# An encoder with four attention mixers in fp32: B's two softmax maps are combined before the transposes, and the small TensorE instructions are issued one at a time between the dense matmuls

## The reference

```python
def block(args):
    qblk, pblk = args
    sc = jnp.einsum('bqmhd,bsmhd->bmhqs', qblk, k) * scale
    dist = jnp.abs(pblk[:, :, None] - posf[:, None, :])
    sc = sc - slopes[None, None, :, None, None] * dist[:, None, None]
    a = jax.nn.softmax(sc, axis=-1)
    a = a[:, 0] - lam[None, :, None, None] * a[:, 1]
    return jnp.einsum('bhqs,bshv->bqhv', a, v)
o = rms_norm(o, subln_g) * (1.0 - lam_init)
```

## Time and profile before

| | us |
|---|---|
| median of 3 runs | 3001.43 |
| lowest and highest | 2998.47, 3010.02 |
| profiled execution, device time | 3004.72 |
| its span | 3002.9 |
| PE busy in it | 2820.7 |
| DVE busy, ACT busy | 1566.0, 1179.0 |
| mean granted TensorE clock | 0.978 |

### The profile page before, as it was taken

One profiled execution on the slowest core, in us unless ns is written; L12 is line 12 of the kernel. 1 busy time (PEld: TensorE's weight loads), 2 busy tenths in 40 slices (PEclk: granted clock), 3 DMA queues, 4 the chain that ended last, 5 costly groups with the idle time before them and its releaser, 6 DMA issues.

```text
span 3002.9 us, 44753 instructions
## 1 busy us (share of the span) xinstructions
PE 2820.7 (94%) x13358; PEld 2267.0 (75%) x13358; DVE 1566.0 (52%) x3238; ACT 1179.0 (39%) x2387; POOL 0.6 (0%) x5
## 2 busy tenths in 40 slices
PE   5999989989989998999979999898899899999998
PEld 4889978666667887888868898776666678788887
DVE  5454476444445445555644544764354454465655
ACT  4444444434433234332434444534444332342432
POOL 0000000000000000000000000000000000000000
PEclk9999999889999999999989999999999999999999
DMA  4212222001112332333332122220111123223332
GB/s 152 72 48 72 78 63 85 12 29 41 45 37 78 94 96 78 99 98 99 99 100 64 44 78 79 67 85 1 36 43 50 31 91 98 92 85 98 95 96 91
DMA packets 141819, 217.62 MB, mean 72 GB/s; under 512 B 14777, under 2 KB 69387, under 8 KB 141195
## 3 DMA queue, kind: packets, MB, share of 16 engines
q1 hardware_dynamic: 132521, 200.62, 21.4%
q10 hardware_dynamic: 9058, 14.06, 1.4%
HBM read 206.20 MB, written 8.45 MB: 71 GB/s over the span
## 4 chain that ended last, share of the span: by engine, by line
PE 81%; DVE 9%; ACT 4%; issue 4%; ACTq 1%; DMA 1%; DVEq 0%; SPq 0%
PE bank L452 21%; PE bank L454 20%; PE bank L453 20%; PE bank L665 7%; PE bank L655 6%; PE bank L503 5%; DVE s_work L1563 1%; DVE s_wl L1139 1%; ACT s_wh L776 1%; ACT s_work L1027 1%; DVE s_work L1294 1%; PE bank L539 1%; ACTq L874 1%; DMA s_raw<-in_w_in 0%; ACT s_work L1019 0%
## 5 line engine op out<-in xcount | busy, mean ns | idle before, releaser
L1139 DVE TENSOR_TENSOR s_wl<-s_raw,s_wh 128x1024 fp32r<-128x1024 f32 (+2 forms) x372 | 453.6, 1220 | 526.5 <-ACT s_wh L776 525.9
L776 ACT ACTIVATE s_wh<-s_raw 128x1024 fp32r<-128x1024 f32 (+2 forms) x372 | 392.2, 1055 | 625.1 <-PE bank L454 591.9
L452 PE MATMUL bank<-s_hTh,s_wh 128*128 128x512 f32 x1216 | 486.2, 400 | 4.5 <-DVE s_work L1231 4.5
L454 PE MATMUL bank<-s_hTh,s_wl 128*128 128x512 f32 x1216 | 476.9, 392 | 0.0
L453 PE MATMUL bank<-s_hTl,s_wh 128*128 128x512 f32 x1216 | 476.7, 392 | 0.0
L452 PE MATMUL bank<-s_wh,s_hTh 128*128 128x512 f32 (+1 forms) x1088 | 475.8, 437 | 0.0
L454 PE MATMUL bank<-s_wh,s_hTl 128*128 128x512 f32 (+1 forms) x1088 | 427.0, 392 | 0.0
L453 PE MATMUL bank<-s_wl,s_hTh 128*128 128x512 f32 (+1 forms) x1088 | 426.7, 392 | 0.0
L1019 ACT ACTIVATE s_work<-s_work,s_stat 128x128 f32<-128x128 f32 (+3 forms) x384 | 214.1, 558 | 369.5 <-DVE s_stat L1588 123.0
L1563 DVE COPY s_work<-bank 128x256 f32<-128x256 f32 (+1 forms) x288 | 105.2, 365 | 394.5 <-ACT s_work L1027 391.9
L503 PE MATMUL bank<-s_consts,s_work 128*128 128x128 f32 (+1 forms) x1560 | 250.0, 281 | 47.3 <-DVE s_gTl L1495 14.3
(11 more groups left out here) (166 smaller groups left out, 3199.6 us busy)
## 6 DMA issues: line engine op xcount, KB each, us to landing
s_raw<-in_w_in SPq DMA_DIRECT2D x168, 512.0 KB, 3.4
s_raw<-in_ffn_w_up SPq DMA_DIRECT2D x176, 256.0 KB, 2.9
s_raw<-in_ffn_w_down SPq DMA_DIRECT2D x44, 512.0 KB, 3.7
s_raw<-in_w_branch SPq DMA_DIRECT2D x32, 512.0 KB, 3.6
s_raw<-in_w_o SPq DMA_DIRECT2D x16, 512.0 KB, 3.6
x_keep<-s_work ACTq DMA_DIRECT2D x2, 2048.0 KB, 7.5
s_raw<-in_w_in SPq DMA_DIRECT2D x16, 256.0 KB, 2.9
s_work<-x_keep ACTq DMA_DIRECT2D x2, 2048.0 KB, 8.2
```

The lines of the kernel that those rows point to most:

```text
L452: mm(out, stationary[0], moving[0], start=start, stop=False)
L454: return mm(out, stationary[1], moving[0], start=False, stop=stop)
L776: a(wh[:, k % 3, 0:n], raw[:, s, 0:n], ACT.Copy).then_inc(*hi_split.up(own))
L1139: v.tensor_tensor(wl[:, k % 3, 0:n], raw[:, k % 2, 0:n], wh[:, k % 3, 0:n].bitcast(F32), ALU.subtract).then_inc(*tile_split.up(own))
```

## The change

It has four parts. B's pairs of maps are combined on DVE: `mixed = p0 + p1 * share`, where `share` is lambda times the ratio of the two row sums; only `mixed` is transposed and multiplied, and one division per tile follows. B's window becomes `gate3a` to four steps before `gate1a` (91 steps instead of 47), and the norm of its output moves behind it. (`attention_b` below is DVE's, and so are the last lines.) The generators on PE now yield before every single dense matmul, transpose and value matmul, and inside an attention step the order is S, T, V. At the start of a layer the first splits of weight tiles move: two ahead of the squares on ACT, one ahead of the norm on DVE, and the others between later steps.

```diff
-    D=(START["Aq"] + 14, START["Bq"], 32), A=(START["Bq"], START["gate3a"], 32), B=(START["gate3a"] + 1, START["gate0a"], 32),
+    D=(START["Aq"] + 14, START["Bq"], 32), A=(START["Bq"], START["gate3a"], 32), B=(START["gate3a"] + 1, START["gate1a"] - 4, 32),
 )
+B_NORM = WINDOW["B"][1]
...
                         for c in range(chunks):
-                            st, mv = operands(b, chunks * i + c, [t[:, c, :] for t in w])
-                            last = split3(PJ[b][:, 0:width], st, mv, i == 0 and c == 0, i == ntiles - 1 and c == chunks - 1)
+                            for st, mv in split3(*operands(b, chunks * i + c, [t[:, c, :] for t in w])):
+                                if n:
+                                    yield START[name] + 4 * i + b + n / (3 * chunks)
...
+            def transposed(dst, sources, done, when, pace, at=0):
+
+                for n, src in enumerate(sources):
+                    if n:
+                        yield when + n * pace
...
+                yield from transposed(TD, sources, td_ready, when, 1 / 6)
...
                     if 1 <= step < n + 1:
-                        yield at + 2 * pace / 3
+                        yield at + 0.1 * pace
...
+                        yield from transposed(TA, [probs[:, u % 2, P * k:P * k + P] for k in range(lo, hi)], ta_ready,
+                                              at + 0.1 * pace, 0.1 * pace, at=lo)
+                    if 2 <= step < n + 2:
+                        yield at + 0.5 * pace
...
+                        for k, (out, st, mv, start, stop) in enumerate(values_of(u, O1, probsT[:, u % 2, :])):
+                            if k:
+                                yield at + (0.5 + 0.06 * k) * pace
+                            last = mm(out, st, mv, start=start, stop=stop)
...
+            def attention_b():
...
+                    if 2 <= step < n + 2 and step % 2 == 0:
+                        yield at + 0.3 * pace
+                        u = step - 2
+                        h, share = (u % 8) // 2, stat[:, 4, 0:1]
+                        p0, p1 = [probs_b[u // 2 % 2][:, m, :] for m in range(2)]
+                        dve.wait_ge(*p_ready.at(l, first + u + 2))
+                        dve.wait_ge(*own.done(l))
+                        v.reciprocal(share, stat[:, 8, u + 1:u + 2]).then_inc(*dve_step.up(own))
+                        dve.wait_ge(*own.done(l))
+                        v.scalar_tensor_tensor(share, share, lam[:, h:h + 1], stat[:, 8, u:u + 1], ALU.mult, ALU.mult).then_inc(*dve_step.up(own))
+                        dve.wait_ge(*own.done(l))
+                        v.scalar_tensor_tensor(mixed[:, u // 2 % 2, :], p1, share, p0, ALU.mult, ALU.add).then_inc(*b_mixed.up(own))
...
+            split_next()
             normalise()
-            for _k in range(3):
-                split_next()
...
+            split_next()
...
-            norm_out(ROW["norm1"])
+            norm_out(ROW["norm1"], split_next)
```

More of the change, by code:

```diff
@@ new lines, in attention @@
+                    if tile_of and step >= 10 and (step - 10) % 8 == 0:
+                        yield at + 0.75 * pace
+                        tile = (step - 10) // 8
+                        pe.wait_ge(*o_out.at(l, outs + tile + 1))
+                        pe.wait_ge(*ta_act.at(l, n_att[0]))
+                        pe.wait_ge(*ta_dve.at(l, n_att[0]))
+                        n_att[0] += 1
+                        yield from transposed(TA, tile_of(tile), ta_ready, at + 0.75 * pace, 0.02 * pace)
@@ L1003, in attention @@
                 for step, at, pace in slots(name):
-                    if tile_at is not None and step >= 11 and (step - 11) % 8 == 0:
-                        yield at + 0.02 * pace
-                        t = (step - 11) // 8
-                        hi_out(gTh[:, tile_at:tile_at + 4, P * t:P * t + P], att_group(), ta_act)
                     if step < n:
@@ L1027, in attention @@
                         a(probsT[:, u % 2, P * lo:P * mid], src[:, P * lo:P * mid], ACT.Copy).then_inc(*ta_act.up(own))
+                    if tile_at is not None and step >= 10 and (step - 10) % 8 == 0:
+                        yield at + 0.82 * pace
+                        t = (step - 10) // 8
+                        hi_out(gTh[:, tile_at:tile_at + 4, P * t:P * t + P], att_group(), ta_act)
+            def attention_b():
+                first, n = n_unit[0], WINDOW["B"][2]
+                n_unit[0] += n
+                for step, at, pace in slots("B"):
+                    if step < n:
+                        yield at + 0.2 * pace
+                        act.wait_ge(*s_biased.at(l, first + step + 1))
+                        if step >= 4:
+                            act.wait_ge(*b_mixed.at(l, step // 2 - 1))
+                        a(probs_b[step // 2 % 2][:, step % 2, :], scores[:, step % 2, :], ACT.Exp, scale=-1.0, bias=stat[:, 5, step:step + 1],
+                          accum_out=stat[:, 8, step:step + 1]).then_inc(*p_ready.up(own))
+                    if 3 <= step < n + 3 and step % 2 == 1:
+                        yield at + 0.52 * pace
+                        pair = (step - 3) // 2
+                        src = att_group()
+                        act.wait_ge(*o_ready.at(l, first + pair - 1))
+                        a(probsT[:, pair % 2, 0:2 * P], src[:, 0:2 * P], ACT.Copy).then_inc(*ta_act.up(own))
             def attentions():
```

194 lines of the change are left out of this document (113 added, 81 removed).

## The result

The changed kernel takes 3015.23 us, the median of 11 runs (3009.58 to 3019.48), where the kernel before took 3001.43 in 11 runs beside it: a ratio of 1.0036 over all runs (1.0046 by the two medians), 95% interval 1.0023 to 1.005. The forecast was 2975, with a range up to 3015: the time moved little, and the other way. The profiled execution has a span of 3016.1 us against 3002.9.

A forecast was written before the change was run, and what follows sets the result against it. PE was taken as the bound (busy 94% of the span, 81% of the chain). Terms -42 + 3 + 50 - 20 - 10 - 9 + 14 - 12 gave -26 us, hence 2975 us by the median; range 2937 to 3015.

The forecast's parts named there:

- (a): B's combination on DVE: fewer transposes and value matmuls save 21 us a layer, 42 in all; DVE's work costed at nothing.
- (d): B's stall behind ACT's parameter DMAs: more queued PE work shortens it, -10 us a layer, -20 in all.
- (e): Other waits in B, for the output bank and for copies: -10 us in all, bounds -14 and 0.
- (g): Turns through the single bank TD: spread transposes make the next turn wait, +7 us a layer, +14 in all.
- (h): Attention outside B, with T ahead of V: shorter waits for copies, -12 us in all, bounds -35 and +20.
- (c): Separation in strided blocks: 191 more small-to-dense places a layer at 0.13 us each, 25 us, 50 in all.
- (b): Separation in contiguous blocks: nothing from separation alone, plus 1.5 us per layer for rounding against it.
- (f): Start of a layer without the early splits: -5 us in the second layer, -4 in the first, -9 together.
- Stalls only move: Rival: B's stall and wait gains and the gain in attention outside B fail; about 3000 us, no change; chance 0.21.
- slower: Rival: spread transposes make PE wait for the single banks TA and TD; +60, 3035 us; chance 0.12.
- Lone instructions cost their stream: Rival: single transposes fall from 0.11 to 0.057 us and strided blocks lose nothing; -140, 2861 us; chance 0.05.

## Why the prediction was wrong

The forecast missed by 40 us. Some 20 lie in the turns of B's normed output, which were priced as if their data were there, and 25 in attention outside B: 12 that were forecast as a gain, 6 that A lost, and 7 in the pause. Some 4 more lie in the rest of B's stretch, and the strided blocks gave back 11.

**(a), (d), (e), B: right in their sum, but the norm was missed.** With the norm out of the way B's stretch is 36.5 and 34.3 us shorter, 71 in both layers, against the 72 of the three terms. Between them the shares lie otherwise than forecast: 27 and 25 come with the combination in the old window (21 was (a)), 9.5 a layer from the window. In the changed kernel the stretch gained only 48.

**(g) failed in one place.** The turns are priced there by their bank alone, 0.3 to 0.8 us each and so 1 to 3 us a layer for the four of B's normed output, and (a) says "I cost DVE's work at nothing"; no term asks when their data is there. It comes from a chain on DVE, and the change put that chain (5.5 us of squares and sums, 2.5 of inverse root, 2.9 of scaling) between the output of `br0b` and splits of weight tiles. "DVE and ACT are idle half the time" is an average over the span: here PE waited for the chain's last instruction. That is about 10 us a layer (33.4 and 34.2 us, where 21.8 and 16 T of 0.11 would be 23.6), 20 of the 24 by which B's stretch missed. PE's own waits are 7.0 of the 10 in the first layer; the rest goes with the lower clock behind them.

Away from `gate1a` the stretches of the turns grew by 15 us against 14, but that agreement is partly luck. Separation alone, from groups to single instructions in the old order, is 1.2 + 2.5 = 3.7 us a layer, 7 in all; 4 came from the order of steps, in `kv` and `cq`; and 4 stand already in the kernel with groups and the old order (180.4 us from `kv` to `br2b` instead of 178.4, mostly in `dq0`), which no run explains.

**(h) failed, in sign.** The prediction said: T now waits for its bank, and the copy stands on ACT behind the next exponential; "I give back 0.1 of the 0.25". The mechanism was seen and priced as a detail. A, forecast at -3 us a layer, lost 2.4 and 3.4. In the three kernels that keep the changed kernel's A (contiguous operand, turns later, strided blocks in sixes) it takes 143.2 to 145.9 us, in the old order 137.7 to 141.8.

In D a unit at full clock did become shorter, from 2.66 to 2.49 us, but the length of the pause followed the clock. The twelve pauses with the order S, T, V and the exponential first take from 125.3 us, at a mean clock of 0.97, to 139.8 at 0.84, though D's instructions are the same; the ten of the old order from 127.5 at 0.96 to 135.0 at 0.88. At 0.96 the new order's are 126.1 and 127.1, the old one's 127.5 to 128.8. So at equal clock the change was worth about 1.5 us a layer, half of what (h) had for D, and the +7 of the table goes with the clock of the two executions that it compares.

The six pauses with the copy first lie apart from all these: 113.6 to 116.3 us at 0.98 to 1.00. So this place on ACT's queue held more than the 35 us that (h) had for its bound, 43 in the changed kernel. The order S, T, V alone was not the fault; it was this order on PE with the exponential ahead of the copy on ACT.

**(c) was right in its mechanism and mis-sized.** The exposed load costs what the rows said, 0.125 us for a place, and the contiguous operand took it away. But the 53 us of (b) and (c) were 42. In the old order, separation costs 21.9 us a layer, 44 in all, with the same rise in places; why it is 2 us a layer less than 191 x 0.125 isn't shown. The rest is the order S, T, V, which takes 0.8 us a layer off the same stretch with single instructions and 3.3 in groups, and which (h) had at nothing. **(b)** costs 0.012 for a place, 2.3 us in the strided stretch of a layer where 1.5 was put for all. **(f)** was -9 and is -9.1.

**The rivals.** *Stalls only move* came nearest in its number (3000), but not by its mechanism: (d) and (e) were won. The *slower* rival asked for over 60 us of transposes waiting for copies, and by the letter of that sign it holds: over all copies out of `TA` and `TD` the list gives 34.2 + 14.4 + 13.8 + 2.7 + 1.2 + 0.8 = 67 us. But 39 of such waits stood in the kernel before (14.3 + 12.4 + 10.8 + 1.9), and V's have fallen by 50; the sign forgot both. The experiments give the spread of the turns 7 us, not 60. *Lone instructions cost their stream* is out: single transposes and groups differ by 0.012, against.

**What stays open.** What decides whether the clock falls in a given pause isn't settled; the same instructions had a mean clock from 0.84 to 0.97. Copy first in the old order of PE wasn't tried, nor B in the old order, and in A the exponential wasn't told apart from the turn's copies and the split that also stood ahead of the copy.

## What to carry to other kernels

When the order of steps changes on one engine, follow the released instruction through the queues of the others: a copy that is ready behind an exponential that isn't waits for all that the exponential waits for, and one edit there (copy first) was worth 43 us in the changed kernel, as much as the combination of B's maps was forecast to bring. Work moved onto an engine that is idle half the time must be read against the queue at its new place, with who waits for its last instruction. Before small instructions are spread between dense ones, count the places and look at what load follows each; with a contiguous stationary operand they cost next to nothing (0.012 us each), with a strided one 0.125 us each. And when a stretch's length follows the clock, compare it with several executions of the same instructions before crediting a change.

## What was new of the hardware

A weight load of 128 columns took 0.31 us when its columns are every fourth of the buffer and 0.19 when they are adjacent, and nearly only behind a short instruction did the difference show in the time between matmuls (0.44 and 0.31 us; behind a long one they are 0.235 and 0.230 us apart).

And the pause, where PE has only small instructions. At the upper level the changed kernel's units take 2.28 and 2.71 us in turn, the longer one with a wait of 0.3, and those with the copy first 2.20. At the end of a tile of eight units, two unit starts are 4.7 to 5.5 us apart in the first and 3.1 to 3.9 in the second. In the changed kernel units of 4.2 to 4.3 us, at the lower of the clock's two levels, follow two such ends of three in the first layer and all three in the second; with the copy first no unit is so long. With the same instructions of D as the changed kernel, the shortest pause was this one, of the kernel with its turns later, in the second layer:

```profile
2029.37:2154.63 125.26, 109.92 (x610) 76.06 (x608) 62.12 (x158) 50.69 (x127) 0.00 (x0) 0.97 0.06 18
```

So of the 20.5 and 21.9 us by which the changed kernel's pauses (134.1 and 135.5) are longer than 113.6, nearly 12 are the waits and what little clock was lost at 0.97, and the remaining 9 and 10 went with the clock, 0.91 and 0.89.
